# A head norm on values centred beforehand, its tiles kept in PSUM, and a bonus gated by GpSimd

## The reference

```python
y = scan(state; r, w, k, v, kk, b)        # state = state*w - (state kk) b^T + v k^T ; y_t = state r_t
mean = jnp.mean(y, axis=-1, keepdims=True)            # over the 64 values of a head
var = jnp.mean(jnp.square(y - mean), axis=-1, keepdims=True)
y = (y - mean) * lax.rsqrt(var + GN_EPS) * ln_w + ln_b
bonus = jnp.sum(rh * kh * r_k, axis=-1, keepdims=True) * vh
y = y + bonus
return (y * jax.nn.silu(gate)) @ w_out
```

## Time and profile before

| what | value |
|---|---|
| median of 3 runs | 1239.25 us (1236.81 to 1241.57) |
| the profiled execution | 1243.05 us, its span 1241.3 us |
| TensorE busy | 1161.3 us, 94% of the span |
| VectorE, ScalarE, GpSimd busy | 61%, 50%, 39% |
| low parts of weights on GpSimd, 128x512, two SBUF inputs | 320, mean 1.37 us |
| v slots | up to 239 us |
| gate slots, and VectorE's inversion | to 287 us, and to 281 us |
| recurrence | 290 to 370 us |
| head norm | 370 to 408 us, overlapping slot 0 of the output product |

### The profile page before, as it was taken

The page is one execution under the profiler, slowest core; times in us unless marked ns, Lnnn a source line. Parts: engine busy times, 40 slices in busy tenths (PEclk is TensorE's granted clock), DMA queues, the critical chain, the costliest instruction groups (busy, mean ns, idle before and its releaser), DMA issues.

```text
span 1241.3 us, 19538 instructions
## 1 busy us (share of the span) xinstructions
PE 1161.3 (94%) x7570; PEld 897.6 (72%) x7570; DVE 753.1 (61%) x1179; ACT 619.9 (50%) x1034; POOL 486.4 (39%) x391
## 2 busy tenths in 40 slices
PE   5899899998886999899999998999999999999987
PEld 5666667787772787677777776877888888867766
DVE  4775997895458436466666655374285234657773
ACT  4666453634553446566556464364221244556655
POOL 1333334357650344333323343443444445532231
PEclk8999899999997899899999999999999999999999
DMA  7742244526213253212222222522333333322111
GB/s 237 248 123 63 58 119 122 166 87 159 51 60 117 67 179 88 83 52 69 68 69 68 68 69 71 166 85 76 95 102 88 99 102 92 95 68 69 51 35 68
DMA packets 198941, 119.49 MB, mean 96 GB/s; under 512 B 27773, under 2 KB 187206, under 8 KB 198598
## 3 DMA queue, kind: packets, MB, share of 16 engines
q1 hardware_dynamic: 196256, 115.95, 32.1%
q10 hardware_dynamic: 2598, 2.33, 0.6%
HBM read 103.06 MB, written 15.20 MB: 95 GB/s over the span
## 4 chain that ended last, share of the span: by engine, by line
PE 41%; issue 30%; POOL 13%; DVE 12%; ACT 2%; DMA 1%; POOLq 0%; SPq 0%; ACTq 0%; DVEq 0%
POOL b_w_lo L562 13%; PE banks L643 10%; PE banks L645 10%; PE banks L644 10%; DVE b_problems L2127 1%; DVE b_sum_squares L2125 1%; PE banks L1218 1%; DVE b_a_lo L1987 1%; PE banks L650 1%; PE banks L891 1%; DVE b_suffix L2576 1%; PE banks L1246 1%; PE banks L910 1%; PE banks L1030 1%; DVE b_sum_squares L2060 1%
## 5 line engine op out<-in xcount | busy, mean ns | idle before, releaser
L562 POOL TENSOR_TENSOR b_w_lo<-b_w_raw,b_w_hi 128x512 fp32r<-128x512 f32 x320 | 430.4, 1366 | 710.7 <-ACT b_w_hi L1316 710.5
L643 PE MATMUL banks<-b_a_lo,b_w_hi 128*128 128x512 f32 x1280 | 524.9, 410 | 24.2 <-DVE b_a_lo L2243 8.6
L645 PE MATMUL banks<-b_a_hi,b_w_lo 128*128 128x512 f32 x1280 | 505.9, 395 | 0.0
L644 PE MATMUL banks<-b_a_hi,b_w_hi 128*128 128x512 f32 x1280 | 505.3, 395 | 0.0
L643 PEld LDWEIGHTS banks<-b_a_lo,b_w_hi 128*128 128x128 f32 x1280 | 244.1, 191 | 103.4 <-issue 21.6
L1316 ACT ACTIVATE b_w_hi<-b_w_raw 128x1024 fp32r<-128x1024 f32 x160 | 168.8, 1055 | 248.3 <-PE banks L645 242.9
L645 PEld LDWEIGHTS banks<-b_a_hi,b_w_lo 128*128 128x128 f32 x1280 | 244.0, 191 | 54.0
L644 PEld LDWEIGHTS banks<-b_a_hi,b_w_hi 128*128 128x128 f32 x1280 | 244.5, 191 | 44.5
L1723 ACT ACTIVATE b_exps<-banks,b_stats 128x128 f32<-128x128 f32 (+3 forms) x64 | 33.2, 524 | 61.3 <-DVE b_stats L2366 61.3
L1657 ACT ACTIVATE b_a_hi<-b_x_t,b_params 128x512 fp32r<-128x512 f32 x48 | 34.0, 719 | 55.5 <-DVE b_x_t L2251 54.9
L2251 DVE TENSOR_TENSOR b_x_t<-b_x_t,banks 128x512 f32<-128x512 f32 x32 | 22.0, 687 | 60.8 <-PE banks L645 60.8
(11 more groups left out here) (314 smaller groups left out, 1508.6 us busy)
## 6 DMA issues: line engine op xcount, KB each, us to landing
b_w_raw<-rw_w_in SPq DMA_DIRECT2D x32, 512.0 KB, 4.3
b_w_raw<-da_w_in SPq DMA_DIRECT2D x32, 512.0 KB, 4.0
b_w_raw<-w_in_a SPq DMA_DIRECT2D x32, 512.0 KB, 4.0
b_w_raw<-pe_w_gate SPq DMA_DIRECT2D x16, 512.0 KB, 4.1
d_ple<-b_ple_out SPq DMA_DIRECT2D x16, 256.0 KB, 4.8
b_w_raw<-rw_w_out SPq DMA_DIRECT2D x8, 512.0 KB, 4.6
b_ple_in<-d_ple SPq DMA_DIRECT2D x2, 2048.0 KB, 10.2
b_w_raw<-da_w_out SPq DMA_DIRECT2D x8, 512.0 KB, 4.1
```

What stands on the lines that cost most here:

```text
L562: m = pool.tensor_tensor(WLO[:, u % 2, ks], WRAW[:, u, ks], WHI[:, u % 2, ks].bitcast(F32), ALU.subtract)
L643: pe.matmul(dst, hi, a_lo[:, k_act, :], start=first, stop=False)
L644: pe.matmul(dst, hi, a_hi[:, k_act, :], start=False, stop=False)
L645: return pe.matmul(dst, lo, a_hi[:, k_act, :], start=False, stop=last)
```

## The change

- v is centred within its head where it is turned: four fp32 products with the centring matrix take the place of the four transposes. As y is linear in v, it comes out centred, and the eight centring products after the recurrence are gone.
- y's last chunk goes to banks 0 and 1, and its state part is issued right after w. Squares and head sums are made in three pieces: chunks 0 to 5 during the last two chunks, chunk 6, chunk 7. VectorE keeps half of the last y.
- rstd is spread by one fp32 product for each tile (before: one fp32r product of two parts in a bank's rows); four of the eight spreads stand between the k tiles of slot 0 of the output product.
- Scaled tiles stay in PSUM: scale, add and gate write their bank, and both parts of the split are read from there. Tiles 0 to 4 have y gated before (part of it in the last chunk) and their bonus gated by GpSimd; tiles 5 to 7 are gated after the sum.
- ln_b is added to the bonus by ScalarE before it is stored. The bonus is loaded back tile by tile into places that come free during the recurrence, and no longer after it.
- The turned blocks lie in weight buffer 2 rather than in the tail region, with a wait of their own; GpSimd's wait for the store moves behind the placements that no longer need it.

```diff
-    (TURNED,) = phase([("turned", [P, BL * BL])], tail_at + BL * BL * 4)
+    TURNED = WRAW[:, 2].rearrange("p k n -> p (k n)")
...
+        sp.wait_ge(sem("u_mm"), 4)
+        for j in range(4):
+            load_bonus(j)
+        sp.wait_ge(sem("u_mm"), 6)
+        for j in range(4, 6):
+            load_bonus(j)
+        sp.wait_ge(sem("s_mm"), 6)
+        for j in range(6, NT):
+            load_bonus(j)
...
-        sp.dma_start(BVT[:, :, :], D_BV.rearrange("j p t -> p j t")).then_inc(sem("gn_in"), 16)
...
+        def gate_bonus(j):
+            pool.wait_ge(sem(f"bonus_in{j // 4}"), 64)
+            pool.tensor_tensor(bonus_home(j), bonus_home(j), GT[:, j, :], ALU.mult).then_inc(sem("bonus_gated"), 1)
+            pool.wait_ge(sem("bonus_gated"), j + 1)
...
-        pool.wait_ge(sem("prob_in"), 48)
+        pool.wait_ge(sem("bonus_v"), NT)
         place_v(in_uv, 1)
         for c in range(NC - 1):
             if c:
                 scale_state(c)
             place_kt(c + 1)
+            if c == 0:
+                pool.wait_ge(sem("prob_in"), 48)
             place_v(in_sv(c + 1), 2 * c + 2)
+            if c == NC - 3:
+                for j in range(3):
+                    gate_bonus(j)
+            if c == NC - 2:
+                gate_bonus(3)
...
+        gate_bonus(4)
...
-            turn_four(BANK[6 - 2 * (j % 2)], [TMP[:, j % 2, t * P:(t + 1) * P] for t in range(TT)]).then_inc(sem("v_turn_mm"), 1)
+            for t in range(TT):
+                m = pe.matmul(bank[:, t * P:(t + 1) * P], TMP[:, j % 2, t * P:(t + 1) * P], cst("center"), start=(t == 0),
+                              stop=(t == TT - 1), skip_group_check=True)
...
+            if c == NC - 1:
+                y_state(c)
+                gn_sums(slice(0, GN_SPLIT), 4, range(4))
...
-            pe.matmul(gn_bank(j), center, YT[:, j, :], start=True, stop=True).then_inc(sem("gn_center"), 1)
...
+        def gn_spread(j):
+            head_spread(BANK[4 + j % 4], SPREADH2, RK2, j).then_inc(sem("gn_bcast"), 1)
...
+            for k in range(NT):
+                pe.wait_ge(sem("act_ready"), A_RWO + k + 1)
+                last = split_product(BANK[0], RUN_RWO[0] % 2, lambda w, k=k: w[:, k, :], k, k == 0, k == NT - 1, 0)
+                if k + 4 < NT:
+                    gn_spread(k + 4)
...
         def bonus_out(j):
             act.wait_ge(sem("bonus_v"), j + 1)
+            own.step(act.activation(TMP[:, 2 + j % 2, :], TMP[:, 2 + j % 2, :], ACT.Identity, bias=prm(LN_B, j)))
             act.dma_start(D_BV[j], TMP[:, 2 + j % 2, :]).then_inc(sem(f"bv_out{j % 2}"), 16)
...
+            if c == NC - 2:
+                act.wait_ge(sem("x_mm"), 2 * NC)
+                act.wait_ge(sem("nk_scaled"), NC - 1)
+                act.wait_ge(sem("y_even"), 2 * (NC - 2))
+                act.wait_ge(sem("y_odd"), 2 * (NC - 2))
+                for j in range(NT):
+                    gn_square(slice(0, GN_SPLIT), j)
...
+        dve.wait_ge(sem("lo_done"), RUN_GATE[0] + NT - 1)
         dve.tensor_copy(TURNED[:, :].rearrange("p (k s) -> p k s", s=BL), blk[:, 0].rearrange("p s t -> p t s")[:, 0:BL, :]
...
+            if c == NC - 1:
+                gate_product(0, slice(0, GN_SPLIT))
+                gate_product(1, slice(0, GN_SPLIT))
+                dve.wait_ge(sem("u_mm"), c + 1)
             keep(UV[up, :, 1, :], tiles(BANK[3][up]), "u_kept")
+            if c == NC - 1:
+                for j in range(2, PREGATED):
+                    gate_product(j, slice(0, GN_SPLIT))
...
-            if k + 4 < NT:
-                gated_bonus(k + 4)
             if k + 2 < NT:
                 gn_scale(k + 2)
             if k + 1 < NT:
                 gn_add(k + 1)
-            split_lo(A_RWO, 0, k, YT[:, k, :])
+            split_lo(A_RWO, 0, k, BANK[4 + k % 4])
+            if PREGATED <= k + 1 < NT:
+                gn_gate(k + 1)
```

More of the change, by code:

```diff
@@ L83, in constant_tables @@
     eps = np.tile(np.array([NORM_EPS, GN_EPS, SUB_EPS, 1.0]), (P, 1))
-    eps = np.concatenate([eps, np.where(low_part, -1.0, 1.0)[:, None], low_part[:, None]], axis=1)
+    eps = np.concatenate([eps, np.where(low_part, -1.0, 1.0)[:, None], low_part[:, None],
+                          np.full((P, 1), 4.0 * GN_EPS)], axis=1)
     parts = [np.eye(P), np.ones((P, P)), np.eye(P) - half / CH, np.where(k <= q, 0.0, NEG),
@@ L280, in emit @@
     SP = ACC[:, :].rearrange("p (j t) -> p j t", t=CH)
[L282 to L286 removed]
+    SPREADH2, RK2 = phase([("spread_heads2", [P, 2, P]), ("gn_rstd", [P, TOK])], nk_at)
+    (GSQ,) = phase([("gn_squares", [P, NT, TOK])], nk_at + FULL)
+    PREGATED = 5
+    GN_SPLIT = (NC - 2) * CH
     AHI2, ALO2 = phase([("a_hi2", [P, NT, TOK], F32R), ("a_lo2", [P, NT, TOK], F32R)], 2 * FULL)
@@ L981, in y_chunk, with gn_sums @@
                 for h in ((0, 1), (1, 0))[j % 2]:
-                    m = pe.matmul(y_at(h, j), UV[:, j, h, :], XR[:, c % 2, j, h, :], start=False, stop=(j >= NT - 2),
+                    m = pe.matmul(y_at(c, h, j), UV[:, j, h, :], XR[:, c % 2, j, h, :], start=False, stop=(j >= NT - 2),
                                   skip_group_check=True)
             m.then_inc(sem("yx_mm"), 1)
+        def gn_sums(cols, squares, tiles=range(NT)):
+            pe.wait_ge(sem("rows_kept"), 6 * (NC - 1))
+            pe.wait_ge(sem("gn_squared"), squares)
+            for j in tiles:
+                m = head_sum(BANK[2][:, cols], GSQ[:, j, cols], j)
+            m.then_inc(sem("gn_mm"), 1)
         for g in range(2):
@@ L1002, in _ @@
             u_of(c)
-            y_state(c)
+            if more:
+                y_state(c)
+            else:
+                gn_sums(slice(0, GN_SPLIT), NT, range(4, NT))
             if more:
@@ L1058, in run_of @@
                 whole_slot(run, j, a0, buf, norm[1] if norm is not None and j == 1 else None)
-        run_of(RUN_RWO, A_RWO, 0)
+        first_out_slot()
+        for j in range(1, NT):
+            whole_slot(RUN_RWO, j, A_RWO, 0)
         run_of(RUN_PE0, A_PE0, 1, norm=norm_rows(16, 4))
@@ L1678, in _ @@
             act.wait_ge(sem("gn_done"), k + 1)
-            split(0, k, YT[:, k, :])
+            split(0, k, BANK[4 + k % 4])
         act.preload_act_table_set("sqrt_and_others")
@@ L2188, in keep, with gate_product @@
             dve.tensor_copy(dst, src).then_inc(sem(done), 1)
+        def gate_product(j, cols):
+            dve.wait_ge(sem("gn_squared"), j + 1 if cols.stop == GN_SPLIT else NT + 2)
+            own.step(stt(out=YT[:, j, cols], in0=YT[:, j, cols], scalar=prm(LN_W, j), in1=GT[:, j, cols], op0=ALU.mult, op1=ALU.mult))
         for g in range(2):
@@ L2213, in _, with gn_gate @@
                 keep_incl(c + 1, 1)
-        for j in range(NT):
-            dve.wait_ge(sem("gn_squared"), j + 1)
-            stt(out=YT[:, j, :], in0=gn_bank(j), scalar=prm(LN_W, j), in1=GT[:, j, :], op0=ALU.mult, op1=ALU.mult
-                ).then_inc(sem("gn_kept"), 1)
-        def gated_bonus(j):
-            own.step(stt(out=BVT[:, j, :], in0=BVT[:, j, :], scalar=prm(LN_B, j), in1=GT[:, j, :], op0=ALU.add, op1=ALU.mult))
+        dve.wait_ge(sem("yx_mm"), NC)
+        for par in range(2):
+            src = BANK[1][(up, low)[par]].rearrange("p (j e t) -> p e j t", e=2, t=CH)
+            keep(YT[up, par::2, (NC - 1) * CH:], src[:, par], "y_odd")
         def gn_scale(j):
+            z = BANK[4 + j % 4]
             dve.wait_ge(sem("gn_bcast"), j + 1)
-            tt(YT[:, j, :], YT[:, j, :], BANK[4 + j % 4], ALU.mult).then_inc(sem("gn_scaled"), 1)
+            if j < PREGATED:
+                tt(z, YT[:, j, :], z, ALU.mult).then_inc(sem("gn_scaled"), 1)
+            else:
+                stt(out=z, in0=YT[:, j, :], scalar=prm(LN_W, j), in1=z, op0=ALU.mult, op1=ALU.mult).then_inc(sem("gn_scaled"), 1)
         def gn_add(j):
+            z = BANK[4 + j % 4]
             dve.wait_ge(sem("gn_scaled"), j + 1)
-            tt(YT[:, j, :], YT[:, j, :], BVT[:, j, :], ALU.add).then_inc(sem("gn_done"), 1)
-        dve.wait_ge(sem("gn_in"), 32)
-        for j in range(4):
-            gated_bonus(j)
-        dve.wait_ge(sem("gn_rstd"), 1)
-        stt(out=RKC2[:, :], in0=RK2[:, :], scalar=IS_LOW, in1=RKS2[:, :].bitcast(F32), op0=ALU.mult, op1=ALU.add
-            ).then_inc(sem("gn_rstd"), 1)
+            if j < PREGATED:
+                dve.wait_ge(sem("bonus_gated"), j + 1)
+            else:
+                dve.wait_ge(sem(f"bonus_in{j // 4}"), 64)
+            tt(z, z, bonus_home(j), ALU.add).then_inc(sem("gn_done" if j < PREGATED else "gn_added"), 1)
+        def gn_gate(j):
+            z = BANK[4 + j % 4]
+            dve.wait_ge(sem("gn_added"), j + 1 - PREGATED)
+            tt(z, z, GT[:, j, :], ALU.mult).then_inc(sem("gn_done"), 1)
+        for j in range(PREGATED):
+            gate_product(j, slice(GN_SPLIT, TOK))
         def split_lo(a0, buf, k, src, scale=None):
```

91 lines of the change are left out of this document (44 added, 47 removed).

## The result

The changed kernel takes 1244.03 us (median of 20 runs, 1240.73 to 1250.32) against 1241.59 for the kernel before, measured beside it (20 runs). The ratio of the two is put at 1.0032, 95% interval 1.0020 to 1.0045: some 4.0 us (2.5 to 5.6) slower; the medians alone are 2.4 us apart. The forecast was 1234.7 and a range of 1229 to 1241; the result lies outside it, on the other side of zero. The profiled execution took 1243.82 (span 1242.0), hardly more than the 1243.05 of before, so the loss has to be read from several traces of each kernel.

What follows compares the result with a forecast made beforehand. From 370 to 408 us ScalarE, TensorE and VectorE were taken to bound the kernel in turns, with the stage before the recurrence also full. +4.2 early and -8.8 in the tail gave -4.6: 1234.7 us, range 1229 to 1241.

Steps and rivals of the forecast that it cites:

- The early part: Ahead of the recurrence: centring turns and ln_b make the first corner product 4.2 us later (3.7 to 6).
- the wait for the four spreads in the tail: Output product's slot 0: VectorE waits for spreads behind TensorE's products, +2.3 us (0.6 at full clock, 4.2 at half).
- The base: Median of 1239.25 us for the kernel before, its profiled 1243.05 being 3.8 above; the forecast change was taken off the median.
- The holes before the splits: Ahead of the gate's splits on ScalarE: ln_b, its wait and the store's issue delay VectorE by about 1.1 and 1.16 us.
- GpSimd's gate products: In the recurrence: GpSimd gates five bonus tiles, about 1.37 us each; three precede a placement, 1.1 late but hidden, cost 0.
- its own signs: Wrong if inversion ends under 2 or over 6 us later, or last y to second residual shrinks under 7 or over 11.
- Step (a): In the v slots: four fp32 centring products replace four transposes, +0.30 us a turn, 1.8 for six (1.7 to 2.9).
- Step (b): Ahead of eight bonus stores: ScalarE adds ln_b, 1.16 us each, partly in gaps; costs 1.1, 1.16 and 0.15 us.
- the two small terms of chunk 7: End of the recurrence: head sums ahead of the u product +0.4 us, VectorE's gate products beside GpSimd +0.5.
- D: Tail: VectorE starts earlier but waits for half-clock spreads, gain 6.4 with 6 lost earlier: -0.4 us, 1238.9; chance 0.08.
- The port: Last chunk: VectorE's gate products beside GpSimd, one step blocked by +1.0, half past its cover, +0.5 us; 1.3 by the skill.
- C: v slots: a centring turn costs far more than 0.81 us; break-even at +1.07 a turn, at +2.1 1245.4 us; chance 0.09.

Runs made afterwards that it cites:

- the early part alone: Kernel before with v's turns as centring products and ln_b added by ScalarE ahead of the bonus stores; ratio 1.0069 (1.0041 to 1.0096) to the kernel before.
- both parts undone: Changed kernel with v turned by four transposes again and ScalarE's ln_b addition left out; ratio 0.9987 (0.9975 to 1.0000) to the kernel before.

## Why the prediction was wrong, step by step

Two terms of the sum failed. The early part, +4.2 in the forecast, measured +5.7 to +7.1, and the wait for the four spreads in the tail, +2.3, measured +6.4. The base, a median of three runs, was 2.3 too low.

**What held.** The holes before the splits (1.16 forecast, 1.17 measured). GpSimd's gate products: three took 3.97 us (4.1 forecast), and the placement that TensorE's w product of the last chunk reads ended at 369.30, 1.5 us before that product at 370.83, which waited 0.67 for VectorE's copy, as in the earlier trace rows. They are hidden.
```profile
368.02 1.28 POOL L592 COPY b_sv<-b_v_stack 64x512 f32<-64x512 f32 x2
```
The end of the recurrence: last y to first scaling forecast as 377.45 - 369.86 = 7.6, measured 7.7 and 7.9, with the four spreads at 2.26 (2.1 forecast). From the last low part to the first residual 1.8 (1.7 forecast).

**By its own signs** it was wrong: the stretch from last y to second residual was to shrink by 7 to 11 us, and it shrank by 5.7 against the trace that the forecast read.

**Step (a), the turn: mis-sized.** Forecast +0.30, from the cheaper of two rows; measured +0.46, near the +0.49 of the dearer one (L1125). Six of them are 2.8 us where the forecast had 1.8. The Trainium skill (TensorE: Matmul & The Clock Gate, Terms) has transpose mode four times faster for fp32; measured is 0.99 against 0.53, 1.9 times, and by an estimate from that page the fp32 products that replace four transposes would take 4 x 0.53 = 2.1. The measurement decides.

**Step (b), ln_b: a wait was missed, which here costs nothing more.** The forecast let it fall in gaps of ScalarE for the first tiles. It fell in a gap of ScalarE, but inside the loop bonus, ln_b, store, landing, bonus of the tile after next, through two places. That alone costs the 2.9 us of the turns, but in parallel with them, so the turns' 2.9 is all that shows in the whole change. To this come its two holes, as forecast: 1.17 + 1.17. Forecast for (a) and (b) up to the last low part: 1.8 + 1.1 + 1.16 = 4.1; measured 5.3 (36.6 to 41.9 from the first bonus), and up to the last y 7.7 by the means of the traces. The other 2.4 us lie in a different place in each trace. In the first the clock stays up behind the hole, the first corner product is 6.1 us late, and the recurrence from there takes 78.7 us, where before has 76.4 to 78.8. In the second the first corner product is 10.9 us late, with half clock and late loads ahead of it, and the recurrence takes 74.5. The kernel with the early part alone repeats this (92.9, then 73.2). With both parts undone the last y is 5.7 us earlier than in the changed kernel, with the early part alone 7.1 later than before: so 5.7 to 7.1 of the 7.7 come from the early part, where the forecast had 4.2, and at most 2.0 from the change in the recurrence, where it had nothing in the sum beyond the two small terms of chunk 7. How the delay grows between the last low part and the last y was not tested. The forecast counted the hole as time of VectorE alone, and TensorE idles behind it too (0.9 before, 2.7 to 2.8 now).

**The tail: the wait for the spreads, mis-sized.** From first scaling to the last low part's start plus its duration the forecast had 19.5 us, of which 2.3 were waits for the four spreads among the products, with the clock back 4.4 us after work becomes dense. It measured 24.1 (383.14 to 407.23), and the waits were 2.01 + 1.69 + 1.64 + 1.03 = 6.4. Two things were off. The clock: work did become dense at 388, by the column of busy time, and it stayed at 0.50 until 410.5; the 4.4 us were the middle of three stretches of before (3.3, 4.3 and 5.7), and here it took 22. And the price at half clock: the forecast had 4.2 for half clock throughout, but its own sizes for a tile, 3.5 us against 1.8 of VectorE's work, were right (3.58 measured), and four such differences are 6.8. In place of the gain of 8.8 stand 5.7 against the first trace of before, and 4.5 by the means; D, which had the spreads at half clock all along, gave 6.4. Between 5.7 and 4.5 lies mainly the clock that the first trace of before lost in its centring products.

What holds the clock down there stays open. It is not the two passes of the fp32 spreads: with fp32r spreads in the same places TensorE was busy 2.00 of 2.00 us in each stretch from 386 to 396, and was granted 0.50 until 404.9. Nor is it settled by their place: with all but one ahead in fp32 the clock rose 6.7 us after the first product (386.76 to 393.5), and of the two kernels with the same spreads ahead in fp32r it rose at 390.3 in the one and at 400.2 in the other. The forecast's reading that each lull of 2 us or more of before was followed by 0.50 does not hold for the whole trace either: behind the 2.81 us ahead of 298.58 the clock stayed at 1.00, and behind the 1.76 ahead of the centring products it fell.

**The port.** For VectorE's gate products beside GpSimd the forecast allowed +0.5. Of the two that ran first, one took 1.02 us and the other 0.62, like the three after them: +0.4, and the last u copy was late by none of it that a row shows. The one of 1.02 lay beside GpSimd's fifth gate product:
```profile
372.08 1.27 POOL L614 TENSOR_TENSOR b_blocks<-b_blocks,b_gate_t 128x512 f32<-128x512 f32 x1
372.75 1.02 DVE L2248 SCALAR_TENSOR_TENSOR b_y_t<-b_y_t,b_params,b_gate_t 128x384 f32<-128x384 f32 x1
```
It ended 0.42 us after GpSimd's (373.35 to 373.77). In the second trace it started earlier, took 1.32 and again ended 0.42 us after. That agrees with the rule of the Trainium skill (SBUF — State Buffer, Terms), that the loser blocks for the whole instruction, as VectorE's inversion steps do (1.64 beside GpSimd, 0.66 alone): in these two traces the cost is what was left of GpSimd's instruction.

**The rivals.** C had the right sign and the right place for a wrong reason: it wanted a turn of +1.07 to break even, and a turn is +0.46. It got 0.09, and slower as a whole 0.05. D's tail got 0.08. No case joined a dear early stage to a tail at half clock throughout, and with the measured 7.7 and 4.5 that is what came.

**Base.** The profiled execution of before was taken as 3.8 above the median, evenly, and the difference carried over. It was not even: against the other two traces 1.8 to 2.5 us of it lay ahead of the last y and 1.6 to 2.9 behind it, in the stretches that the change rebuilds, and 1.9 to 3.9 came back after the second residual. A stretch of one trace says what that execution did, to some 2 us. The median itself was that of three runs, 1239.25; twenty runs of the same kernel gave 1241.59. So 2.3 of the 9.3 us between 1234.7 and 1244.03 are the base, and as a difference -4.6 was forecast and +4.0 measured.

## What to carry to other kernels

Where an instruction is added between a producer and its store, follow the buffer round to its next writer: its time and the later issue count there, also when the engine that runs it has gaps (here 2.8 us at the fifth bonus). When two parts each lengthen a different loop to the same event, take the larger, and expect that undoing one of them shows nothing at that event. Put no small product that another engine waits for between the products that it releases; where there is room, issue them all ahead (here 5 us). And before costing a stretch off one trace, read a second one: stretches of 45 to 75 us differed by 2 to 3 us between executions of one kernel.

## What was not expected of the hardware

TensorE, busy 2.00 of 2.00 us in every stretch from 388 to 402, was granted 0.50 all that time, while fp32 spreads of 32 rows (2.07 us for two instructions) alternated with 128x512 products. In the kernel before, TensorE was busy from 394 with no gap over 0.3 us until 399.4, and the clock was up at 400; in its third trace, the same instructions, it rose only at 403.

ScalarE's four issues of the turned blocks' loads took 2.05 us in most traces, but 2.3 to 8.0 in four of the five whose gate slots had run at half clock. In the second trace of the changed kernel, to which this row of two of the four belongs, all four took 8.05 us, and the loads landed 6.1 us after issue rather than 3.0 (medians):
```profile
289.90 3.99 ACTq L1612 DMA_DIRECT2D b_blocks_turned<-d_turned  x2
```
What filled the queues there was not examined.
